# A head's 56 level differences computed on DVE instead of POOL, in a chunked gated recurrence

## What is computed

```
def chunk_recurrence(q, k, v, log_a, s0):
    """S_t = diag(a_t) S_{t-1} + k_t v_t^T ; o_t = S_t^T q_t, chunkwise."""
    ...
        b = jnp.cumsum(la, axis=2)
        rel = b[:, :, :, None, :] - b[:, :, None, :, :]
        decay = jnp.exp(jnp.where(causal, rel, -jnp.inf))
        ...
            scores = jnp.einsum('bhtsd,bhsd->bhts', qc[:, :, :, None, :] * decay, kc)
        out = (jnp.einsum('bhts,bhsv->bhtv', scores, vc)
               + jnp.einsum('bhtd,bhdv->bhtv', qc * jnp.exp(b), state))
```

## Time and profile before

| | us |
|---|---|
| median of 3 runs | 3029.99 |
| lowest and highest | 3023.05, 3030.07 |
| profiled execution | 3031.0 |
| its span | 3029.3 |
| TensorE busy | 2765.9 (91%) |
| its weight loads | 2241.9 (74%) |
| DVE busy | 2002.4 (66%) |
| ACT busy | 1384.6 (46%) |
| POOL busy | 509.0 (17%) |

### The profile page before, as it was taken

How to read it: one execution, slowest core, us unless ns; L and a number is a source line. 1 busy time by engine, 2 the same in 40 slices (tenths; PEclk the granted TensorE clock), 3 DMA queues, 4 the chain that set the end, 5 groups by cost and what they waited for, 6 DMA issues and landing times. The chain is left out here.

```text
span 3029.3 us, 40819 instructions
## 1 busy us (share of the span) xinstructions
PE 2765.9 (91%) x13693; PEld 2241.9 (74%) x13694; DVE 2002.4 (66%) x2174; ACT 1384.6 (46%) x1448; POOL 509.0 (17%) x437
## 2 busy tenths in 40 slices
PE   6898998989857949999999999999999999999993
PEld 6577685867846838777778787878878877787773
DVE  4245161543656649789996969686676677967774
ACT  3132131322253427567764746454454455745552
POOL 0032330323200322111111212011110121101110
PEclk9999999999978969999999999999999999999997
DMA  8402002020053269789996978686676687958763
GB/s 340 152 9 65 15 22 67 11 77 4 22 194 111 77 220 350 257 295 356 354 345 206 364 249 308 232 281 204 195 240 229 195 289 260 370 187 290 273 227 132
DMA packets 292638, 611.49 MB, mean 202 GB/s; under 512 B 30462, under 2 KB 78246, under 8 KB 289394
## 3 DMA queue, kind: packets, MB, share of 16 engines
q1 hardware_dynamic: 268020, 565.14, 52.4%
q0 software_dynamic: 20384, 43.19, 6.4%
q10 hardware_dynamic: 4160, 2.10, 0.2%
HBM read 585.09 MB, written 49.59 MB: 210 GB/s over the span
## 5 line engine op out<-in xcount | busy, mean ns | idle before, releaser
L1795 DVE TENSOR_TENSOR e_slot_r<-e_slot,whi 128x2048 fp32r<-128x2048 f32 x296 | 674.4, 2285 | 129.1 <-ACT whi L1735 129.1
L1735 ACT ACTIVATE whi<-e_slot 128x2048 fp32r<-128x2048 f32 x296 | 560.9, 1912 | 376.5 <-PE e_acc L1646 376.5
L1646 PE MATMUL e_acc<-whi,e_xlo 128*128 128x512 f32 x1600 | 634.5, 397 | 0.0
L1644 PE MATMUL e_acc<-whi,e_xhi 128*128 128x512 f32 x1600 | 633.8, 396 | 0.2
L1735 ACT ACTIVATE whi<-slot 128x2048 fp32r<-128x2048 f32 x148 | 282.9, 1911 | 189.7 <-PE e_acc L1646 189.7
L1795 DVE TENSOR_TENSOR slot_r<-slot,whi 128x2048 fp32r<-128x2048 f32 x151 | 345.1, 2288 | 20.3 <-ACT whi L1735 17.6
L1646 PEld LDWEIGHTS e_acc<-whi,e_xlo 128*128 128x128 f32 x1600 | 300.4, 188 | 73.4
L1644 PEld LDWEIGHTS e_acc<-whi,e_xhi 128*128 128x128 f32 x1600 | 301.2, 188 | 65.4 <-DVE e_slot_r L1795 3.2
L346 PE MATMUL h_pj<-slot,uT 128*128 128x128 f32 (+1 forms) x2304 | 329.9, 304 | 10.8 <-DVE h_gate L719 6.0
L346 PEld LDWEIGHTS h_pj<-slot,uT 128*128 128x128 f32 x2304 | 307.8, 191 | 30.6 <-issue 8.6
L1644 PE MATMUL e_acc<-whi,e_ahi 128*128 128x512 f32 x800 | 322.2, 403 | 0.0
(11 more groups left out here) (281 smaller groups left out, 3483.8 us busy)
## 6 DMA issues: line engine op xcount, KB each, us to landing
e_slot<-in_w SPq DMA_DIRECT2D x296, 1024.0 KB, 6.8
slot<-in_w SPq DMA_DIRECT2D x151, 1024.0 KB, 6.3
slot<-in_w_ada SPq DMA_DIRECT2D x24, 1024.0 KB, 6.9
slot<-in_w_in SPq DMA_DIRECT2D x28, 512.0 KB, 6.5
projected<-h_stage SPq DMA_DIRECT2D x56, 128.0 KB, 1.7
r_vqk<-projected SPq DMA_DIRECT2D x4, 1280.0 KB, 7.5
xt<-in_x SPq DMA_DIRECT2D x8, 512.0 KB, 8.5
slot<-in_w_out SPq DMA_DIRECT2D x4, 1024.0 KB, 15.2
```

Of the source, the lines that this page charges most:

```text
L1644: pe.matmul(out, hi[:, k, c], wh, start=False, stop=False)
L1646: return pe.matmul(out, lo[:, k, c], wh, start=False, stop=last)
L1735: act.activation(whi[i % RING][:], raw[i % PIECES][:], ACT.Copy).then_inc(S["whi_made"], 1)
L1795: v.tensor_tensor(wlo[i % PIECES][:], raw[i % PIECES][:], whi[i % RING][:].bitcast(F32), ALU.subtract).then_inc(S["wlo_made"], 1)
```

## The change

The loop over the levels with its four subtractions leaves POOL's program and is put, unchanged, into DVE's `levels(half)`: ahead of L733 and of all products of that half, 28 in a row. It still adds to `lev_sub` one by one, and ACT's waits are the same. For the first half DVE gets one more wait, for POOL's third subtraction of the head (`pool_sub`), which `cum[1]` and `qdec[1]` need; the wait on `s_done` was there for the products already and now stands ahead of the run.

```diff
@@ POOL @@
-                for half in range(2):
-
-                    g.wait_ge(S["s_done"], h * LT + half * HT)
-                    for l, hl in enumerate(LEVELS):
-                        nb = HN // (2 * hl)
-                        view = lambda x: x.rearrange("p (b f n) -> p b f n", f=2, n=hl)
-                        fwd, bwd = (view(cum[d][:, CTX + half * HN:CTX + (half + 1) * HN]) for d in range(2))
-                        k4, q4 = view(wk[:, l, :]), view(wq[:, l, :])
-
-                        mf = fwd[:, :, 0, hl - 1:hl].to_broadcast((P, nb, hl))
-                        mb = bwd[:, :, 1, 0:1].to_broadcast((P, nb, hl))
-                        for out, x, y in ((k4[:, :, 0], mf, fwd[:, :, 0]), (k4[:, :, 1], bwd[:, :, 1], mb),
-                                          (q4[:, :, 0], mb, bwd[:, :, 0]), (q4[:, :, 1], fwd[:, :, 1], mf)):
-                            g.tensor_tensor(out, x, y, ALU.subtract).then_inc(S["lev_sub"], 1)
@@ DVE @@
                 def levels(half):
                     lo = half * HN
+                    if half == 0:
+                        v.wait_ge(S["pool_sub"], h * 3 + 3)
                     v.wait_ge(S["s_done"], h * LT + half * HT)
                     k0, k1 = (key[d][:, CTX + lo:CTX + lo + HN] for d in range(2))
+                    for l, hl in enumerate(LEVELS):
+                        ...
+                        for out, x, y in ((k4[:, :, 0], mf, fwd[:, :, 0]), (k4[:, :, 1], bwd[:, :, 1], mb),
+                                          (q4[:, :, 0], mb, bwd[:, :, 0]), (q4[:, :, 1], fwd[:, :, 1], mf)):
+                            v.tensor_tensor(out, x, y, ALU.subtract).then_inc(S["lev_sub"], 1)
                     c.did(v.tensor_tensor(wk[:, NL, :], k0, k1, ALU.add))
                     for l, hl in enumerate(LEVELS):
                         ...
```

More of the change, by code:

```diff
@@ L730, in levels @@
                     lo = half * HN
+                    if half == 0:
+                        v.wait_ge(S["pool_sub"], h * 3 + 3)
                     v.wait_ge(S["s_done"], h * LT + half * HT)
                     k0, k1 = (key[d][:, CTX + lo:CTX + lo + HN] for d in range(2))
+                    for l, hl in enumerate(LEVELS):
+                        nb = HN // (2 * hl)
+                        view = lambda x: x.rearrange("p (b f n) -> p b f n", f=2, n=hl)
+                        fwd, bwd = (view(cum[d][:, CTX + half * HN:CTX + (half + 1) * HN]) for d in range(2))
+                        k4, q4 = view(wk[:, l, :]), view(wq[:, l, :])
+                        mf = fwd[:, :, 0, hl - 1:hl].to_broadcast((P, nb, hl))
+                        mb = bwd[:, :, 1, 0:1].to_broadcast((P, nb, hl))
+                        for out, x, y in ((k4[:, :, 0], mf, fwd[:, :, 0]), (k4[:, :, 1], bwd[:, :, 1], mb),
+                                          (q4[:, :, 0], mb, bwd[:, :, 0]), (q4[:, :, 1], fwd[:, :, 1], mf)):
+                            v.tensor_tensor(out, x, y, ALU.subtract).then_inc(S["lev_sub"], 1)
                     c.did(v.tensor_tensor(wk[:, NL, :], k0, k1, ALU.add))
```

## The result

3038.43 us (median of 8 runs, 3032.23 to 3041.85) against 3029.35 (8 runs, 3023.05 to 3031.45) beside it: ratio 1.0031, 95% interval 1.0020 to 1.0042. The change costs some 9 us of 3029; the forecast was 3035 in a range of 3023 to 3047. At 0.31% the loss is small but clear of zero, and just over the 9 us that the prediction took for the least that can be told from no change. The profiled execution took 3038.51 us, its span is 3036.9.

What follows compares the result with a forecast made beforehand. TensorE was taken to bound the recurrence, idle 18 us a head. Per head +2.7 + 1.65 - 2.2 - 1.65 = +0.5 us; four heads +2, two more clock falls +3.3: +5 us, so 3035 us, range 3023 to 3047.

Steps and rivals of the forecast that it cites:

- The price: Cost of one moved 128x256 subtraction on DVE: 0.337 us, taken from half-wide products of the same size and strides.
- rival 1: DVE's broadcast subtractions can't overlap and stand 0.42 us apart: +6.5 us a head, 3056 us; chance 0.08.
- First half: Differences ahead of DVE's products make ACT's copies late, so TensorE idles 3.9 us instead of 1.2: +2.7 us a head.
- the slow clock: TensorE's granted clock falls to 0.50 behind idle time: 1.65 us a head charged in the first half, regained in the second.
- Second half: TensorE's wait for the last product before the scores goes, -2.2 us a head, and its slow clock, -1.65.
- The forecast margin of 0.2 us: Second half: levels ready at 265.4, TensorE done with its projections at 265.63, so it goes on without a wait.
- The term of 2.2 us: Second half: TensorE's wait for the last product of the levels disappears, -2.2 us in every head.
- Sum: Whole kernel: +0.5 us a head, +2 in four heads, +3.3 for two clock falls before the second half's second output: +5.
- Rival 2: Clock falls at both remaining TensorE gaps in all heads, or stays low longer: +8 to +14 us, 3038 to 3044; chance 0.20.
- Rival 3: No clock fall behind either remaining TensorE gap: -1.2 us a head, 3025 us; chance 0.18.
- Rival 4: First half not late because TensorE's projections cover ACT: -3.9 us a head, 3014 us; chance 0.04.

Runs made afterwards that it cites:

- The half alone: Only the second half's 28 differences on DVE, the first half's left on POOL, against the kernel before: 3021.23 us, ratio 0.9968.
- the lengthened run: The changed kernel plus three useless 128x256 subtractions on DVE behind the second half's differences: 3042.84 us, ratio 1.0044 to the kernel before.
- the first half alone: Only the first half's 28 differences on DVE, the second half's left on POOL, against the kernel before: 3049.92 us, ratio 1.0060.
- the copies between the exponentials: The changed kernel with two of ACT's projection copies moved between the first half's exponentials: 3036.75 us, ratio 1.0021 to the kernel before.
- the fastest kernel: Changed kernel with first-half differences in DVE's idle time, two ACT copies between exponentials, task 12's projection in TensorE's 2.64 us wait: 3001.88 us, 0.9905 of the kernel before.

## Why the prediction came out as it did

- The price. 0.335 us a subtraction, as taken from L738 (0.337). The broadcast operand costs nothing, so rival 1 is out. The Trainium skill ("GPSIMD Engine Reference", section "Elementwise — side-by-side cycle accounting") has a ratio of 1.96 between the engines, which would have given 0.30; the ratio measured here is 1.75.
- First half. ACT was 2.64 us late (2.7 forecast), TensorE's idle time 3.86 (3.9), the slow clock behind it cost 1.64 to 1.71 (1.65), in all 4.3 a head as forecast. Leaving it on POOL or moving it forward takes exactly this away. DVE's wait for the states is 2.48 us where I said 0.9: the slow clock, which I charged on TensorE, also gave DVE its 1.6 us.
- Second half. The wait and its slow clock are gone, 3.9 us a head as forecast, though in other parts: 2.33 us of wait (2.2 in the sum) and 1.57 of slow clock (1.65). The half alone shows it. The forecast margin of 0.2 us was hardly there: the levels came when forecast, but the scores started 0.15 us behind the last product, a step that the sum left out, and the lengthened run puts the margin at 0.03. The term of 2.2 us was right, and close to being less.
- Sum. A grew by 1.9 us in four heads (2 forecast), B by 3.3 (3.3 forecast, and in two heads of four). That this last number is exact is luck: in how many heads the clock falls there differs between kernels with the same work in that place, 0 of 4 heads before, 2 of 4 in the changed one and in three of the variants, 4 of 4 in four others.
- Short of the measured 9 us are 4. In the profiles 1.9 of them lie between a head's start and A. The prediction had no term for a fourth place of slow clock, the head's start; as shown above, the low clock lasted longer there and accounts for all of the 1.9. It also makes the heads 183.4, 181.7 and 183.8 us apart, two of them beyond the forecast 181.5 to 183. Why the clock rose later was not tried. Ahead of the first A lie 0.6 us more (TensorE's first products of the recurrence start at 118.73 instead of 118.04), for which no cause was sought, and the 1.6 us by which the medians differ more than the two profiled executions can't be placed.
- Rival 2 named 3038 to 3044, and the measured number is its number, but the profile does not show its mechanism: the first half's fall cost what was charged, and the second came in two heads, not four. In other executions it may have come in more. Rival 3 (no fall behind either gap) is out by the fall behind 3.86 us in all four heads. Rival 4 (ACT covered by projections) was wrong for the reason given: nothing was to spare.

The choice that carried the forecast was to follow ACT's program and not DVE's. By DVE's alone the first half's products end at 227.7, only 1.8 us behind the old start of the states at 225.89, because 6.9 us of idle time cover most of the run. One would have charged 1.8 us a head, no fall of the clock, and forecast a gain of some 8 us instead of a loss (estimate: four times 1.8 less 3.9).

## What to carry to other kernels

When work goes to another engine, its new place is set by what stands ahead of it in that engine's program, and its consumers' programs decide what it costs: here the run had 12 us of idle time two steps earlier, and from the place it was given it held up copies on a third engine that TensorE wanted. Try the halves of such a change apart; one was worth -9 us and the other +19. A wait of two to four microseconds on TensorE cost its length here and in many heads 1.3 to 2.9 us more, so it paid to put ready, independent products into it.

## What the runs showed of the hardware

- Whether the clock falls behind a wait of TensorE is not set by the wait's length alone. Behind 3.7 to 3.9 us it fell in all heads of all kernels that had it; behind 2.2 us in seven of the eight heads of the kernel before and of the first half alone; behind 2.64 us in none of the kernel before and in two or four heads of others, with the same work around it (in one of these heads, with the first half alone on DVE, the wait was 2.04 us); behind 0.4 to 1.5 us never. It can fall behind 1.92 us too: in the first head of the kernel before, the last four products (L562) take 1.06 us instead of 0.61. A fall behind a wait of 2.2 us or more cost 1.3 to 2.9 us, or 0.7 where it set in while TensorE was still waiting (the first head with the copies between the exponentials). The Trainium skill ("TensorE: Matmul & The Clock Gate", section "What's actually happening") says that the window in which the chip watches TensorE's activity runs freely and isn't reset when a kernel starts. That would explain the same wait with and without a fall; no run here was made to show it.
- Heads differ where the clock falls in some and not in others: A and B together vary by 2.9 us between the heads of the kernel with the second half alone on DVE. Where the falls are the same in every head they agree, whether there are none (0.03 us, the fastest kernel) or some (0.02 us, the longer run, with two falls in each head).
- A pair of DVE subtractions that starts beside one of POOL's takes longer than alone (the first pair above, 2.47 us instead of 0.75). The Trainium skill ("SBUF — State Buffer", section "SBUF: two separate sides") describes a port pair that one of the two engines holds for a whole instruction while the other waits. That fits the trace: POOL's subtraction lasts from 181.16 to 183.53, and the pair, begun at 181.68, ends 0.6 us behind it.
